# A two-block network in fp32: the second block's branch gates and projections put beside the next branch's attention, the residual kept in DRAM, another norm chain

## What is computed

```python
h = rmsnorm(x_first, final_norm_w)                      # the first block's last step
hn = rms_norm(h, ln_gain)
z = split_columns(hn @ w_in + b_in)
y_a = rglru_branch(z['lru_x'], ...) * silu(z['lru_gate'])         # a recurrence over the tokens
y_b = nsa_branch(q_b, k_c, v_c, k_s, v_s, k_w, v_w, g_b) * silu(z['nsa_gate'])
y_c = fox_branch(rms_norm(q), rms_norm(k), v, log_f) * silu(z['fox_gate'])
mg = sigmoid(z['merge']).reshape(b, s, 3, 2048)
merged = (mg[:, :, 0] * (y_a @ w_branch[0]) + mg[:, :, 1] * (y_b @ w_branch[1])
          + mg[:, :, 2] * (y_c @ w_branch[2]))
h = h + merged @ w_out
h = h + sigmoid(h @ w_ple_gate) * rms_norm(p @ w_ple, ple_gain)
```

## Time and profile before

| | |
|---|---|
| median of 3 runs | 3529.06 us (3529.05 to 3529.77) |
| the profiled execution | 3528.45 us, of it a span of 3526.6 us |
| PE busy | 3301.3 us (94%) |
| PE weight loads busy | 2940.5 us (83%) |
| DVE busy | 2389.8 us (68%) |
| ACT busy | 1416.6 us (40%) |
| POOL busy | 29.1 us (1%) |
| chain that ended last | PE 68%, DVE 17%, DVE's sequencer 4%, ACT 4%, DMA 3% |
| DMA | 684.51 MB, mean 194 GB/s |

### The profile page before, as it was taken

One profiled execution on the slowest core, in us unless ns is written; L12 is line 12 of the kernel. 1 busy time (PEld: TensorE's weight loads), 2 busy tenths in 40 slices (PEclk: granted clock), 3 DMA queues, 4 the chain that ended last, 5 costly groups with the idle time before them and its releaser, 6 DMA issues.

```text
span 3526.6 us, 50514 instructions
## 1 busy us (share of the span) xinstructions
PE 3301.3 (94%) x21371; PEld 2940.5 (83%) x21371; DVE 2389.8 (68%) x2934; ACT 1416.6 (40%) x1333; POOL 29.1 (1%) x12
## 2 busy tenths in 40 slices
PE   7999999999999999799999999698998899999999
PEld 2788989989988887687888788587897889998887
DVE  1686567778777877777666555676685566846756
ACT  1333645534444343333333333253444534453333
POOL 0000000000000000100000000200000000000000
PEclk9999999999999999899999999899999899999999
DMA  8786544466444756566555555344544255434544
GB/s 361 292 308 241 189 162 168 165 230 251 167 166 173 294 205 237 191 251 239 188 183 191 175 189 185 126 161 144 179 168 171 73 190 179 168 126 173 182 167 155
DMA packets 100468, 684.51 MB, mean 194 GB/s; under 512 B 10927, under 2 KB 14063, under 8 KB 24980
## 3 DMA queue, kind: packets, MB, share of 16 engines
q1 hardware_dynamic: 93024, 655.04, 51.2%
q10 hardware_dynamic: 7220, 26.25, 2.0%
HBM read 674.86 MB, written 9.53 MB: 194 GB/s over the span
## 4 chain that ended last, share of the span: by engine, by line
PE 68%; DVE 17%; DVEq 4%; ACT 4%; DMA 3%; issue 2%; POOL 0%; ACTq 0%; POOLq 0%; SPq 0%
PE accp L443 29%; PE accp L444 15%; PE accp L448 5%; PE accp L450 5%; PE accp L449 5%; DVE wlo L1336 4%; PE accp L446 2%; DMA mraw_a<-wm 2%; DVEq L1403 2%; DVE cv L1581 2%; ACT whi L930 1%; DVEq L1580 1%; DVE macc L1401 1%; DVE hrec L1375 1%; DVE macp L1401 1%
## 5 line engine op out<-in xcount | busy, mean ns | idle before, releaser
L1336 DVE TENSOR_TENSOR wlo<-raw,whi 128x2048 fp32r<-128x2048 f32 (+1 forms) x544 | 1202.9, 2214 | 462.0 <-ACT whi L930 457.7
L930 ACT ACTIVATE whi<-raw 128x2048 fp32r<-128x2048 f32 (+1 forms) x544 | 1002.0, 1846 | 737.4 <-DMA raw<-w 692.5
L443 PE MATMUL accp<-act,whi 128*128 128x512 f32 x3075 | 1101.0, 400 | 33.1 <-POOL act L414 18.5
L444 PE MATMUL accp<-act,wlo 128*128 128x256 f32 x3280 | 890.2, 282 | 0.0
L448 PE MATMUL accp<-act,whi 128*128 128x256 f32 x2768 | 807.2, 292 | 31.4 <-POOL act L414 27.0
L449 PE MATMUL accp<-act,whi 128*128 128x256 f32 x2768 | 788.8, 285 | 0.0
L450 PE MATMUL accp<-act,wlo 128*128 128x256 f32 x2768 | 788.8, 285 | 0.0
L443 PEld LDWEIGHTS accp<-act,whi 128*128 128x128 f32 x3075 | 580.6, 189 | 170.7 <-DVE tf L1346 12.6
L444 PEld LDWEIGHTS accp<-act,wlo 128*128 128x128 f32 x3280 | 622.3, 190 | 19.1
L448 PEld LDWEIGHTS accp<-act,whi 128*128 128x128 f32 x2768 | 537.1, 194 | 40.5 <-issue 30.8
L449 PEld LDWEIGHTS accp<-act,whi 128*128 128x128 f32 x2768 | 537.2, 194 | 5.8 <-issue 5.3
(11 more groups left out here) (434 smaller groups left out, 3472.0 us busy)
## 6 DMA issues: line engine op xcount, KB each, us to landing
raw<-w SPq DMA_DIRECT2D x480, 1024.0 KB, 4.8
mraw_a<-wm SPq DMA_DIRECT2D x52, 1024.0 KB, 7.5
raw<-w SPq DMA_DIRECT2D x64, 704.0 KB, 4.0
mraw_b<-wm SPq DMA_DIRECT2D x24, 1024.0 KB, 7.0
mraw_c<-wm SPq DMA_DIRECT2D x16, 1024.0 KB, 6.9
acb<-ac_d ACTq DMA_DIRECT2D x8, 1024.0 KB, 4.6
mraw_w<-wm SPq DMA_DIRECT2D x4, 1024.0 KB, 7.6
bw_d<-br_d ACTq DMA_DIRECT2D x4, 768.0 KB
```

What stands on the lines that cost most here:

```text
L443: pe.matmul(acc, wh, both, start=first, stop=False, skip_group_check=True)
L444: mm = pe.matmul(acc[:, 0:S], wl, x2[:, 0, :], start=False, stop=False, skip_group_check=True)
L930: act.activation(whi[:, c % 4, 0:k, :], raw[:, c % 4, 0:k, :], ACT.Copy).then_inc(hi_done, 1)
L1336: dve.tensor_tensor(wlo[:, c % 4, 0:k, :], raw[:, c % 4, 0:k, :], whi[:, c % 4, 0:k, :].bitcast(F32), ALU.subtract).then_inc(lo_done, 1)
```

## The change

Seven edits are made together.

1. The block's phases are put in another order: `lx`, `lg`, `bf`, `nq`, `cmp`, `bra` (24), `ng`, `fx`, `brb` (24), `fg`, `brc` (24), `w2`, `ple`, `pg`. A `br*` phase is made of triples: gate chunk, gate chunk, and one projection chunk for the same two output tiles. Two chunks of `bra` stand in front of the first attention, and the other 22 ride in its 12 batches (two in each of ten, one in each of the last two); 16 of `brb` ride in the second attention (four in each batch), 8 follow it. `ng` and `fg` follow the attentions.
2. Gates are taken by ACT from PSUM (narrow form) with the sigmoid in the same instruction; projections are narrow too, and DVE multiplies PSUM by the gate directly. `proj`, `gate`, `branch`, `merge` go. DVE gates the attention's output tile by tile (`gated`).
3. The first three `lx` chunks are run together (`triple`): for each quarter of the input PE works on all three, in three accumulators.
4. The norm chain: the root of the product is taken directly (one reciprocal, one root and one Newton step ahead of the first quarter instead of two each), and `x2T` is no longer written between the quarters.
5. DVE instead of POOL makes `act_lo` of the four quarters.
6. `x1r` is stored to DRAM (`x1f_d`, 2 MB) by a DMA from ACT's queue at the start of the norm chain; ACT waits for the store before it overwrites the third quarter. It is loaded again into `x2T` (2 MB) ahead of `brc`, and scaled there, two tiles after each triple.
7. The 16 modulation pieces ride on every fourth `fi` chunk instead of every second.

The buffers of the recurrence and of the head norms move to other places. The diff, cut:

```diff
-    ("lx", 8, 8), ("lg", 8, 8), ("wba", 8, 16), ("mga", 16, 16),
-    ("bf", 1, 1), ("nq", 20, 20), ("cmp", 8, 2), ("ng", 8, 8), ("wbb", 8, 16), ("mgb", 16, 16),
-    ("fx", 24, 24), ("fg", 8, 8), ("wbc", 8, 16), ("mgc", 16, 16),
+    ("lx", 8, 8), ("lg", 8, 8), ("bf", 1, 1), ("nq", 20, 20), ("cmp", 8, 2), ("bra", 24, 32),
+    ("ng", 8, 8), ("fx", 24, 24), ("brb", 24, 32), ("fg", 8, 8), ("brc", 24, 32),
...
-        RIDES = {b: [b + 1] for b in range(1, 7)} | {NSA_B + b: [2 * b, 2 * b + 1] for b in range(4)}
+        RIDES = {b: [2 * b + 2, 2 * b + 3] for b in range(10)} | {10: [22], 11: [23]}
+        RIDES |= {NSA_B + b: [4 * b + n for n in range(4)] for b in range(4)}
...
-                               (19, C0["wo"] + 2, 4, 2), (20, C0["fi"] + 4, 16, 2)):
+                               (19, C0["wo"] + 2, 4, 2), (20, C0["fi"] + 4, 16, 4)):
...
-            for m in range(8, 12):
-                lo_quarter(m, accM)
...
+            def triple(c, e, n):
+                pe.wait_ge(*out_of(e))
+                for q in range(4):
+                    pe.wait_ge(quarter_lo, 4 * n + q + 1)
+                    for i in range(3):
+                        if q == 0:
+                            pe.wait_ge(lo_done, c + i + 1)
+                        for k in range(4 * q, 4 * q + 4):
...
+            def branch_chunk(ph, n):
+                c, e = C0["br" + ph] + n, E0["br" + ph] + n // 3 * 4 + n % 3
+                if n % 3 < 2:
+                    chunk(c, e, acts)
+                    return
...
+                halves(c, e, rhs, 8)
...
+            act.wait_ge(rq, 3)
+            act.dma_start(x1f_d, x1r[:, :, :].rearrange("p k n -> p (k n)")).then_inc(x1f_st, 16)
             warm_root()
-            root(3, sqF[:, 3, :], sqF[:, 0, :])
-            root(4, rstd[:, :], sqF[:, 4, :])
+            root(3, rstd[:, :], stat[:, 2, :])
+            root(4, root3[:, :], stat[:, 3, :])
             for n in range(8, 12):
+                if n == 10:
+                    act.wait_ge(x1f_st, 16)
                 hi_quarter(n, accM)
...
+            def branch_take(ph, n):
+                split_hi(C0["br" + ph] + n + 1)
+                if n % 3 < 2:
...
+                    take(C0["br" + ph] + n, E0["br" + ph] + n // 3 * 4 + n % 3, tm2[:, m % 4, :], ACT.Sigmoid,
+                         bias=C("b2", B2["mg" + ph] + m))
...
+            act.wait_ge(yb_ok, 16)
+            act.dma_start(x2T[:, :, :].rearrange("p k n -> p (k n)"), x1f_d).then_inc(x1_in, 16)
...
+            normed(0)
+            for m in range(1, 4):
+                normed(m)
+                low_quarter(7 + m, accM)
+            low_quarter(11, accM)
             dve.wait_ge(rs, 4)
+            newton(root3[:, :], v3, tmp)
...
+            def branch_post(ph, n):
+                split_lo(C0["br" + ph] + n + 1)
+                if n % 3 == 2:
+                    for h in range(2):
...
+                        dve.wait_ge(*out_of(e - 1))
+                        dve.wait_ge(used, 2 * (C0["br" + ph] + n) + h + 1)
+                        dve.tensor_tensor(o, acc_of(e), tm2[:, m % 4, :], ALU.mult).then_inc(summed, 1)
+                        if ph != "a":
+                            dve.drain()
+                            dve.tensor_tensor(o if ph == "c" else accM[:, m, :], o, accM[:, m, :], ALU.add)
+                        if ph == "c":
+                            dve.drain()
+                            ins = pair(m2_hi[:, m, :], m2_lo[:, m, :], o)
...
+                if n % 3 == 2:
+                    for k in range(n // 3 * 2, n // 3 * 2 + 2):
+                        dve.scalar_tensor_tensor(x2T[:, k, :], x2T[:, k, :], C("fin", k), root3[:, :], ALU.mult, ALU.mult)
```

More of the change, by code:

```diff
@@ L303, in first_and_second_block @@
         SH0, _p = {}, 0
-        for name, n in (("ga", 16), ("fi", 44), ("mga", 16), ("mgb", 16), ("mgc", 16), ("pg", 16)):
+        for name, n in (("ga", 16), ("fi", 44), ("pg", 16)):
             SH0[name] = _p
@@ L433, in chunk @@
                     first, last = start and k == 0, stop and k == nk - 1
-                    mm = product(accp[:, e % 2, :], wh, wl, x2, first, last, wide)
+                    mm = product(acc_of(e), wh, wl, x2, first, last, WIDE[e])
                     if k == 7 or k == nk - 1:
@@ L810, in _ @@
             mm.then_inc(hct_mm, 1)
-            chunk(C0["ng"], E0["ng"], acts)
+            branch_chunk("a", 0)
             pe.wait_ge(cw2_in, 16)
@@ L901, in _ @@
                     transposes([fx[:, c - 2, :], fx[:, c - 1, :]], c // 2 - 1)
-            attention(NSA_B, len(BATCH), "fg")
-            branch("c", 9)
+            attention(NSA_B, len(BATCH), "b")
+            for n in range(16, 24):
+                branch_chunk("b", n)
+            for c in range(8):
+                chunk(C0["fg"] + c, E0["fg"] + c, acts)
+            for n in range(24):
+                branch_chunk("c", n)
             merged2 = lambda k: m2_2[:, k]
             pe.wait_ge(m2_ok, 1)
-            sixteen("w2", merged2, late(merged2, 15, acts_ok, 10))
+            sixteen("w2", merged2, late(merged2, 15, acts_ok, 8))
             pe.wait_ge(p_ok, 1)
@@ L1284, in attention @@
                                    ACT.Copy).then_inc(aC, 1)
-            attention(0, NSA_B, "ng")
-            act.wait_ge(acts_ok, 8)
-            branch("b")
+            attention(0, NSA_B, "a")
+            for t in range(8):
+                gate_take("ng", t)
             split_hi(C0["fx"] + 1)
-            act.wait_ge(mgb_ok, 1)
+            act.wait_ge(yb_ok, 8)
             for c in range(25):
```

270 lines of the change are left out of this document (132 added, 138 removed).

## The result

The changed kernel took 3484.05 us (median of 4 runs, 3478.91 to 3485.03), beside 3529.06 for the kernel before; the ratio is 0.9871, with a 95% interval from 0.9859 to 0.9882. The forecast was 3474.5, so the change won 45 us where I had forecast 54.5. The profiled execution is the quickest of its four: 3478.91, with a span of 3477.1 at a mean granted clock of 0.978. The other three, at 0.976, took 3483.95 to 3485.03. Span against span the change won 49.5 us.

The account below looks back on a forecast made before the run. PE was taken as the bound, busy 94% of the span. Terms 17.8 + 3.5 + 6.6 + 27.9 + 2.5 + 4.2 - 8.0 = 54.5 us won gave a median of 3474.5 us, own range 3463 to 3486 (3460 to 3504 with 0.8).

Parts of the forecast that it names:

- Pieces: Stage `fi`: modulation pieces on every fourth chunk remove the whole loss to DVE's two-chunk loop, 17.8 us won, lower bound 10.
- Norm chain and triple: Start of `lx`: PE starts earlier, then stands 9 us on the third chunk's split; 3.5 us won, bounds 0 and 9.
- Cover for the recurrence: `bf` and `nq` run during the recurrence, but the wait moves to the softplus; 6.6 us won, bounds 4 and 10.
- The first attention: 22 `bra` chunks ride in its 12 batches and cover its waits, the other engines keeping up; 27.9 us won, bounds 20 and 34.
- The second attention: Chunks of `brb` and `fg` behind it remove the wait for the gated output; 2.5 us won, bounds 0 to 4.
- `w2`: Start of `w2`: the last tiles are finished sooner after PE, so its first chunk waits less; 4.2 us won, bounds 2 to 4.4.
- The narrow form: 48 gate and 24 projection chunks cost PE 0.11 us more each; 8.0 us lost, bounds 6 and 9.
- The residual through DRAM: The 2 MB store at the norm chain and reload ahead of `brc` were taken as hidden, 7.9 us each, at no cost.
- my second rival: `br*` triples: late weights delay ACT's `whi`, DVE's split and product; all 24 lose 2.6 us or more, 3578 us; chance 0.06.
- a small stall at each triple: `br*` triples: weights landing in 8 us cost 1.2 us at each of 24, 29 us in all, 3503 us; chance 0.12.
- the triples stall: `br*` triples: late weights make all 24 lose 2.6 us or more, kernel slower, 3578 us at 11 us landings; chance 0.06.
- Less is won in the attention: Attention batches: engines waiting for one another in order set the pace, 24 us of the gain go, 3498 us; chance 0.17.

Follow-up runs that it names:

- the control: The changed kernel unaltered, timed once more beside later versions to see how far its time and stages repeat: 3483.46 us, ratio 0.9874 to the kernel before.
- the version with all three edits: The changed kernel without the triple, with the chunk ahead of the values in one-chunk batches and the softplus late in one piece: 3463.02 us, ratio 0.9817.
- four versions that close the gap: Changed kernel with the chunk ahead of the values in one-chunk batches: alone 3478.0 us; also without the triple, softplus early 3464.04, late whole 3463.02, late in parts 3458.57.

## Why the prediction came out as it did

The direction and the order of the terms were right and the time was inside the range; the forecast was 9.5 us too good. Its steps, each against the stages of the changed kernel:

- **Pieces: 17.8 forecast, 14.6 when tried alone, 13.3 between the two profiles.** The loop over four chunks does fit, as worked out. The size was off because I took all that the stage had above its pace for DVE's loop, and 2.8 of it is PE's own work on four blocks of the modulation.
- **Norm chain and triple: 3.5 forecast, 4.6 measured (5.1 in the control).** The new side came as worked out: PE starts 17.4 us after `fo` (17.7 forecast), stands for 8.6 us on the third split (9 forecast), and the fourth chunk takes 8.17 us. What the forecast did not ask is what this order costs against the order without the triple. Two runs say 11 to 12 us: the shorter chain and DVE's quarters are worth about 16.5 (83.0 to 66.5), and the triple loses over two thirds of that. One reading of the old side was wrong. I had given each of POOL's quarters a fourth of the 19.55 us, 4.9, and so PE's start at 2258.4. It started at 2264.2:

```profile
2264.20 0.55 PE L448 MATMUL accp<-act,whi 128*128 128x256 f32 x1 [25.07 <-POOL act L414]
```

  The first quarter alone took 10.6 us, for DVE ran its stream of multiplies until 2261.9 (last section). PE thus starts 14 us earlier than before, not 8. The sum was spared, since the end of the old stage was read from a row.
- **Cover for the recurrence: 6.6 forecast.** Above their pace `wba`, `bf` and `nq` lost 29.6 us before, and `bf` and `nq` lose 20.8 now (22.1 in the control): 8.9 won, or 7.5. The wait did move to the softplus, 6.3 us where I had 7.1. From the last `lg` chunk the next four took 37.7 us where I had 39.6; the old side, 17.9 and 5.5, was 23.4 where I had 23.2. Six further `nq` chunks stand 0.8 to 1.4 above the pace, before and after alike.
- **The first attention: 27.9 forecast, 19.3 measured. This step failed.** From the end of the second `bra` chunk to the first `ng` matmul 171.9 us were forecast and 180.5 came, with 53.8 above the pace instead of 45.2. Behind the first, the batches with two chunks are about as worked out, 13.7 to 15.4 us each; five of them lie up to 0.4 above the 15 us that I had named as a sign of being wrong. Four places make nearly all of the rest. The first chunk of the stretch is 15.77, 0.4 over. The 19 chunks behind it are 3.0 over PE's own work, 2.1 of it two waits for DVE's product (L1902). The two batches with one chunk took 21.8 us, 3.7 above their work. And the first `ng` chunk lost 2.3 instead of 0.7. I had asked whether each engine fits into a batch with two chunks, 14.6 us. A batch with one has 9.0, and there the order on ACT, table, eviction, copy, is the path. Against a slow chain I had set the five batches of the earlier trace rows, which had one chunk each and lost nothing; but there the table load stood ahead of the wait, and in the changed kernel it stands behind it. And I had put the clock's cost at nothing for waits under 4 us: with waits of at most 1.9, the two batches ran at 0.84 to 0.92 and took 3 us more than in two versions at 1.00. Turning PE's order around won 6.5 of these 8.7 us. The waits in it, some 3.5 us, are shown by this; that the other 3, the clock, follow from the order is not, since two versions with the old order had full clock as well.
- **The second attention: 2.5 forecast, 3.5 measured.** **`w2`: 4.2 forecast, 3.3 measured.** Right in kind.
- **The narrow form: -8.0 forecast.** All `brc` chunks but one are 5.76 apart, against 5.65 for the wide form before: the 0.11 stands for these 24. The other 48 mostly run beside the attentions, where it can't be read. The 2.5 ns a matmul that the Trainium skill (TensorE: Matmul & The Clock Gate, section "Wait — 56ns, not 53.3ns?") gives beyond the columns would be, as an estimate, 0.04 a chunk; the trace doesn't agree, and the row decides. (The prediction has the sum 5 us lower by that page. It is the time that would be lower; the sum of what is won would be 5 us higher.)
- **The residual through DRAM: nothing forecast, 1.3 lost.** One `brc` chunk took 7.04 us. PE waits there 1.0 us for DVE's product, which stands behind a split, which stands behind ACT's `whi`, which waits for its weight:

```profile
ACT whi L964 <- DMA raw<-w: 2.4, 2, 1.6
```

  That is the chain of my second rival, and it made one triple 18.6 us, above the 17.5 that I had named. ACT waits for weights in the later triples too (2.4 to 5.3 us in a triple) and nothing is lost there, so this row alone isn't the sign. What is particular is the DMA: its share is 0.69 in 3127 to 3155 and 0.51 behind it, and the reload took 9.8 us to land, where I had 7.9. Over the ten traces with the reload the chunk goes with it: 6.84 us where it landed in 9.3, 7.04 with 9.8, 7.70 with 10.5, and 9.71 with 11.3 (the version with all three edits). That the reload causes it is argued from this and from its place; I did not try the kernel with the reload elsewhere.

The parts of the rivals: "a small stall at each triple" and "the triples stall" came at one triple of `brc` alone, all its other chunks are 5.76 apart. "Less is won in the attention" came in part, 8.6 of its 24 us, and by single places, not by a pace of the chain.

Profile against profile the change won 49.5 us, 5.0 fewer than forecast. Short of it were the attention (8.6), the pieces (4.5), the reload (1.3) and `w2` (0.9), together 15.3; above it were the recurrence (2.3), the norm (1.1) and the second attention (1.0), 4.4. The remaining 5.9 us in the change's favour come from stages for which nothing was forecast, 2.4 of them ahead of `fi`, where no edit reaches. In the control these same stages took 3.2 us more than in the kernel before, not 2.4 less. That is repeat, not gain, and it is most of what lies between the profile's 49.5 and the medians' 45.0.

## What to carry to other kernels

When a stall is found inside a new step, ask at once what the old order would cost now that the other edits are in: here a forecast that had the stall to half a microsecond still missed that dropping the step, or making one weight split earlier, was worth 11 us. Work that has slack on average can still be too long in one piece: moved whole, the softplus moved its wait with it; cut into parts of at most 3.4 us behind the regular splits it cost nothing in its stage, though some came back in the next ones. And when filler work runs out before the batches do, look at the last batches by themselves: the order that is harmless with two chunks beside it can be the path with one, and the trace of an older version clears it only if ACT's table load stands on the same side of the wait there. Last, don't spread one record of four instructions evenly: POOL's 19.55 us were 10.6, 2.3, 4.4 and 2.3.

## What the runs showed of the hardware

**DVE and POOL hold each other up, and whole instructions at a time.** Beside POOL's four quarters, DVE operations of 0.29 to 0.43 us took 2.3 to 2.4. The events of the semaphore `quarter_lo`, which each quarter raises, say when it was done: 2239.21, 2241.72, 2244.09 and 2246.59. The three long DVE operations end at 2239.48, 2241.86 and 2244.36, each 0.1 to 0.3 us behind a quarter. The other way round, DVE's multiply stream, which ran when POOL started (16 in 6.42 us), kept its 0.40 each, and POOL's first quarter was done only 6.1 us after its start, 2.6 behind the stream's end; the other three took 2.4 to 2.5. In the kernel before the quarters were done at 2264.07, 2266.40, 2270.75 and 2273.08: the first 2.2 us behind the end of DVE's stream, the third after 4.4 us, across DVE's split, which itself took 3.76 us instead of 2.29, and the others after 2.3. In the first block of the changed kernel, where POOL's quarter begins first, at 1442.65, it takes 2.34, and DVE's operation on 128x4 elements that begins at 1442.70 takes 2.31, where the same took 0.16 just before. So an undisturbed quarter is 2.3 us and not 4.9. The Trainium skill (SBUF — State Buffer, section "Who interferes with whom") says that for a pair of ports the two engines share, the one that issues second waits for the other's whole instruction; that the loser changes with the order agrees with both traces, and so do the ends of the three DVE operations. That POOL waited for the whole stream of multiplies, and not for one of them, is what these traces add.

**The same work at two clocks.** In the last two batches of the first attention the same instructions ran with PE equally busy (8.05 of 10 us) at different granted clocks. First the changed kernel, then the version with the late softplus:

```profile
2700.00:2710.00 10.00, 8.05 (x56) 7.81 (x55) 3.68 (x8) 6.01 (x9) 0.00 (x0) 0.84 0.28 97
```

```profile
2700.00:2710.00 10.00, 8.05 (x67) 7.69 (x66) 3.73 (x9) 7.50 (x14) 0.00 (x0) 1.00 0.31 120
```

At 0.84 part of the window ran at 1.2 GHz, and a batch took 10.9 us; at 1.00 it took 9.4. The changed kernel, its control and two other versions had 10.9, two versions had 9.4. Since the control repeated 10.9 and the two with 9.4 differ ahead of this place, it stays open whether this is chance or follows from the moment at which the stretch begins. The four versions that close the gap have 7.1 and 7.4 us for the last two chunks, all alike, and in the first of them the clock stayed at 1.00 here. So it fell in four of six traces with the gap and in none of four without; that it takes the gap to fall is likely by this, not shown. They are also most of what the versions without the triple and with the late softplus won beyond their own stages (`bra` 190.4 and 190.3 instead of 193.6).
